# One more half of an FFN by Strassen's quarter products, and the modulation sums laid out anew over three FFNs

## What is computed

```python
cond = jax.nn.silu(c)
for i in range(DEPTH):
    mod = (cond @ ada_w[i] + ada_b[i]).reshape(b_, N_SUBLAYERS, 3, D_MODEL)
    h = adaln(x, norm_g[i, 0], mod[:, 0, 0], mod[:, 0, 1])
    x = x + 0.5 * (1.0 + mod[:, 0, 2][:, None, :]) * swiglu(h, ffn_w_in[i, 0], ffn_w_out[i, 0])
    ...
def swiglu(h, w_in, w_out):
    g, u = jnp.split(h @ w_in, 2, axis=-1)
    return (jax.nn.silu(g) * u) @ w_out
```

## Time and profile before

| | |
|---|---|
| median of three runs | 2896.82 us |
| profiled execution | 2896.0 us |
| its span | 2893.6 us (2.4 us lie around it) |
| PE busy | 2873.8 us (99%) |
| DVE busy | 1939.4 us (67%) |
| ACT busy | 1264.7 us (44%) |
| granted TensorE clock, mean | 0.999 |

### The profile page before, as it was taken

One profiled execution on the slowest core, in us unless ns is written; L12 is line 12 of the kernel. 1 busy time (PEld: TensorE's weight loads), 2 busy tenths in 40 slices (PEclk: granted clock), 3 DMA queues, 4 the chain that ended last, 5 costly groups with the idle time before them and its releaser, 6 DMA issues. The chain is left out here.

```text
span 2893.6 us, 40922 instructions
## 1 busy us (share of the span) xinstructions
PE 2873.8 (99%) x16099; PEld 2485.7 (86%) x16099; DVE 1939.4 (67%) x2624; ACT 1264.7 (44%) x1752; POOL 144.9 (5%) x297
## 2 busy tenths in 40 slices
PE   8999999999999999999999999999999999999999
PEld 7888889899898998868999988788888888888887
DVE  8667688777786777876856758766535467754453
ACT  4223255344452445474533445654414348443332
POOL 0111100100001001040000000200000001000000
PEclk9999999999999999999999999999999999999999
DMA  7867613524236243251332322413232222232231
GB/s 299 272 217 255 210 45 115 206 109 154 89 115 230 91 168 107 88 182 61 108 126 79 114 91 88 160 63 110 87 105 98 95 81 95 96 108 95 88 109 66
DMA packets 100944, 366.99 MB, mean 127 GB/s; under 512 B 11248, under 2 KB 11808, under 8 KB 100784
## 3 DMA queue, kind: packets, MB, share of 16 engines
q1 hardware_dynamic: 77616, 276.56, 27.9%
q0 software_dynamic: 23168, 88.17, 8.8%
HBM read 362.51 MB, written 2.18 MB: 126 GB/s over the span
## 5 line engine op out<-in xcount | busy, mean ns | idle before, releaser
L1263 DVE TENSOR_TENSOR wl<-raw,wh 128x1024 fp32r<-128x1024 f32 x393 | 477.1, 1226 | 519.4 <-ACT wh L697 518.9
L697 ACT ACTIVATE wh<-raw 128x1024 fp32r<-128x1024 f32 x393 | 409.8, 1054 | 752.4 <-PE PS L2131 685.1
L2131 PE MATMUL PS<-HH,wh 128*128 128x512 f32 x1560 | 608.2, 390 | 0.4 <-DVE HL L1979 0.3
L2131 PE MATMUL PS<-HL,wh 128*128 128x512 f32 x1560 | 607.7, 390 | 0.0
L2131 PE MATMUL PS<-HH,wl 128*128 128x512 f32 x1560 | 607.7, 390 | 0.0
L2131 PEld LDWEIGHTS PS<-HH,wh 128*128 128x128 f32 x1560 | 293.1, 188 | 62.1 <-DVE HL L1979 0.8
L2131 PEld LDWEIGHTS PS<-HH,wl 128*128 128x128 f32 x1560 | 293.0, 188 | 60.5
L2131 PEld LDWEIGHTS PS<-HL,wh 128*128 128x128 f32 x1560 | 293.1, 188 | 60.3
L2131 PE MATMUL PS<-AH,wh 128*128 128x512 f32 x848 | 330.7, 390 | 0.5 <-DVEq L2014 0.5
L2131 PE MATMUL PS<-AL,wh 128*128 128x512 f32 x848 | 330.5, 390 | 0.0
L2131 PE MATMUL PS<-AH,wl 128*128 128x512 f32 x848 | 330.3, 390 | 0.0
(11 more groups left out here) (346 smaller groups left out, 5107.6 us busy)
## 6 DMA issues: line engine op xcount, KB each, us to landing
raw<-in_stream SPq DMA_DIRECT2D x459, 512.0 KB, 3.4
acc<-in_stream POOLq DMA_DIRECT2D x54, 512.0 KB, 4.9
WK<-in_stream SPq DMA_DIRECT2D x42, 512.0 KB, 4.5
piece<-in_stream POOLq DMA_DIRECT2D x38, 512.0 KB, 5.0
WK<-in_stream POOLq DMA_DIRECT2D x24, 512.0 KB, 6.6
arena<-in_stream SPq DMA_DIRECT2D x16, 512.0 KB, 12.5
HT<-in_stream POOLq DMA_DIRECT2D x12, 512.0 KB, 6.8
TBa<-negcum POOLq DMA_DIRECT2D x8, 640.0 KB, 5.0
```

The source lines that it names most:

```text
L697: F(wh[:, r, :], raw[:, r, :], ACT.Copy).then_inc(hi_done, 1)
L1263: TT(wl[:, r, :], raw[:, r, :], wh[:, r, :].bitcast(F32), ALU.subtract).then_inc(lo_done, 1)
L2131: mm = MM(PS[g % 2][:, j, :], l, x, start=(first and i == 0), stop=(last and i == 2), skip_group_check=after_halves)
```

## The change

The second half of the first FFN (`gate=0`) makes its five groups of the first map by quarter products. The mixtures of its input are made by ACT and DVE during the first half's groups 2 to 5 (`u` in the code), in `arena`, `acc`, `HT` and the places in `TH`, `TL` and `HH`/`HL`.

The 128 modulation sums are divided anew. The first FFN makes 64: 32 in groups 2 to 5 of the first half (two after each split), 22 in that half's output projection (three after each split), 10 in the second's (two after each split). The FFNs with gates 2 and 3 make 32 each, 22 and 10. The first 32 sums use a ring of three tiles in `WK` and `piece`, all others the ring of four. The second half's groups of the first FFN have no sums.

Small moves go with it: the broadcast condition vector `condc` lives in `bands` until the end of the first FFN, so the load of the pooling bands is issued there by SP and not at the start; the scratch of two small reductions is `SG` instead of `WK`.

```diff
--- before.py
+++ after.py
@@ -76,13 +76,13 @@
 
-FAST = {2: (4, 5), 3: (4, 5), 5: (4, 5)}
-
-ADA_BY = {0: 8 + 3 * NADA, 2: 8 + 4 * NADA, 3: 8 + 5 * NADA}
-
-ADA_EARLY = ADA_BY[0]
-
-ADA_PHASES = (16, 8)
+FAST = {0: (0, 5), 2: (4, 5), 3: (4, 5), 5: (4, 5)}
+
+ADA_EARLY = 32
+
+ADA_PHASES = (22, 10)
+
+ADA_BY = {0: ADA_EARLY + 32, 2: ADA_EARLY + 64, 3: ADA_EARLY + 96}
 
@@ -178,6 +178,7 @@
                                             tile=2 * (ng - nf), sums=ADA_BY[f["gate"]] - ADA_PHASES[1] if late else 0))
+                    st["at"][half] = st["parts"][-1]
                 add["fs"] += 7 * nf
@@ -283,7 +284,7 @@
                     *(WK[:, 2 * i:2 * i + 2, :].rearrange("p k t -> p (k t)") for i in range(2))]
-        ada_tiles = [acc[:, 1, 1024:2048], acc[:, 1, 2048:3072], piece[:, 0:1024]]
+        ada_tiles = [ada_late[2], ada_late[3], ada_late[0]]
 
@@ -330,9 +331,13 @@
 
-        def mix_raw(i):
-
-            o = 2048 + 1024 * i + (2048 if i >= 4 else 0)
+        def mix_raw(i, sets):
+
+            if sets == 0 and i == 7:
+                return HT[:, :, :].rearrange("p a (b t) -> p (a b) t", b=2)
+            if sets == 0 and i >= 4:
+                return acc[:, 1, 1024 * (i - 4):1024 * (i - 3)].rearrange("p (k t) -> p k t", k=4)
+            o = ((4096, 5120, 10240, 11264)[i] if sets == 0 else 2048 + 1024 * i + (2048 if i >= 4 else 0))
             return arena[:, o:o + 1024].rearrange("p (k t) -> p k t", k=4)
@@ -590,6 +594,11 @@
                     loaded = part["c"] + RING
+                if st is plan[2]:
+                    load_chunks(loaded, part["c"] + st["halves"][1][1] + 1)
+                    loaded = part["c"] + st["halves"][1][1] + 1
+                    sp.wait_ge(cond_moved, 1)
+                    sp.dma_start(bands[:, 0:NBAND], A["params"][:, NCOL:NCOL + NBAND]).then_inc(bands_in, 16)
             load_chunks(loaded, NCH)
@@ -611,15 +620,18 @@
             pl.memset(ones[:, :], 1.0).then_inc(ones_done, 1)
-            pl.wait_ge(ada0_step, 14)
+            pl.wait_ge(ht_done, KT)
             for m, (s, j) in enumerate(ADA_ORDER[:ADA_EARLY]):
...
             for st in plan:
-                for part, n in zip(st.get("parts", ()) if st.get("gate") in ADA_BY else (), ADA_PHASES):
-                    pl.wait_ge(a_ready, part["e"] + part["n"] + 1)
+                for part, n in zip(st["at"] if st["kind"] == "ffn" and st["gate"] in ADA_BY else (), ADA_PHASES):
+                    if part:
+                        pl.wait_ge(a_ready, part["e"] + part["n"] + 1)
+                    else:
+                        pl.wait_ge(mix_ready, 4)
                     for i in range(n):
@@ -888,7 +900,7 @@
                 act.wait_ge(mix_sum, 4 * sets + i + 1)
-                src = mix_raw(4 + i)
+                src = mix_raw(4 + i, sets)
                 if i < 3:
@@ -1003,7 +1014,11 @@
                                 split_until(c + 4 * u + 8)
+                                if u == 4:
+                                    for i in range(3):
+                                        mix_high(i, st["sets"])
                                 hidden_group(st, e + u, g + u, c + 4 * (u + 1), cv + u, j + u, 2 * u, 0)
+                            mix_high(3, st["sets"])
                             e, cv, g, c, j, pairs = e + ng, cv + ng, g + ng, c + 4 * ng, j + ng, 0
@@ -1025,6 +1040,9 @@
                                 split_until(c + nt // 2 + RING)
+                                if st is plan[2] and c + nt == c_last:
+                                    act.wait_ge(ada_step, ADA_BY[0])
+                                    F(condb, condc, ACT.Copy).then_inc(cond_moved, 1)
                             c += nt // 2
@@ -1621,22 +1639,25 @@
-            def whole(k, t, i):
-
-                link(TT(mix_raw(i), quadrant(HH, k, t).bitcast(F32), quadrant(HL, k, t).bitcast(F32), ALU.add))
-
-            def mixed_input(i, a, b, op):
+            def whole(k, t, i, sets):
+
+                link(TT(mix_raw(i, sets), quadrant(HH, k, t).bitcast(F32), quadrant(HL, k, t).bitcast(F32), ALU.add))
+
+            def mixed_input(i, sets):
...
-                if op is None:
-                    STT(mix_raw(4 + i), a, -1.0, b, ALU.mult, ALU.subtract).then_inc(mix_sum, 1)
+                if i >= 2:
+                    dve.wait_ge(mix_sum, 4 * sets + (1 if i == 2 else 3))
+                a, b = (mix_raw(k, sets) for k in ((0, 1), (1, 2), (4, 2), (3, 6))[i])
+                if i == 2:
+                    STT(mix_raw(4 + i, sets), a, -1.0, b, ALU.mult, ALU.subtract).then_inc(mix_sum, 1)
...
-                    TT(mix_raw(4 + i), a, b, op).then_inc(mix_sum, 1)
+                    TT(mix_raw(4 + i, sets), a, b, ALU.add if i == 3 else ALU.subtract).then_inc(mix_sum, 1)
...
-                src = mix_raw(4 + i)
+                src = mix_raw(4 + i, sets)
@@ -1773,51 +1794,62 @@
...
-                        if ada and not st["parts"]:
-                            paired = st is plan[2] and c == st["c"]
-                            if paired:
-                                split_until(c + 10)
-                                hidden_group(st, e, g, cv, j, 0, 0)
-                                split_until(c + 11)
-                                hidden_group(st, e + 1, g + 1, cv + 1, j + 1, 2, 0)
-                                split_until(c + 12)
-                                e, cv, g, c, j = e + 2, cv + 2, g + 2, c + 8, j + 2
-                            for u in range(2 if paired else 0, ng):
+                                fast_groups(st, part, None)
+                            e, cv, g, c, j, ng = e + ng, cv + ng, g + ng, part["c"], j + ng, 0
+                        elif st is plan[2]:
+                            split_until(c + 10)
+                            hidden_group(st, e, g, cv, j, 0, 0)
+                            split_until(c + 11)
+                            hidden_group(st, e + 1, g + 1, cv + 1, j + 1, 2, 0)
+                            split_until(c + 12)
+                            e, cv, g, c, j = e + 2, cv + 2, g + 2, c + 8, j + 2
+                            for u in range(2, ng):
                                 for i in range(4):
                                     split_until(c + RING + 1 + i)
-                                    n = (2 if i < 3 else 1) if st is plan[2] else 1 if i < 3 else 2
-                                    ada_until(min(ada, at["ada"] + n))
+                                    ada_until(at["ada"] + 2)
+                                    if (u, i) == (2, 1):
+                                        whole(0, 0, 0, sets)
+                                        whole(0, 1, 1, sets)
+                                        mixed_input(0, sets)
+                                    elif (u, i) == (2, 3):
+                                        whole(1, 1, 2, sets)
+                                    elif (u, i) == (3, 1):
+                                        mixed_input(1, sets)
+                                        mixed_input(2, sets)
+                                    elif (u, i) == (3, 3):
+                                        whole(1, 0, 3, sets)
+                                        mixed_input(3, sets)
+                                    elif u == 4 and i:
+                                        mix_low(i - 1, sets)
                                 hidden_group(st, e, g, cv, j, 2 * u, 0)
                                 e, cv, g, c, j = e + 1, cv + 1, g + 1, c + 4, j + 1
-                            ada_until(min(ada, at["ada"] + 1))
-                            if paired:
-                                late_constants()
-                        pairs = 0 if ada or st["parts"] else ng // 2
+                            mix_low(3, sets)
+                            late_constants()
+                        pairs = 0 if part or st is plan[2] else ng // 2
                         with dve.Fori(0, pairs) if pairs else nullcontext(0) as it:
                             for u in range(2) if pairs else ():
                                 base = at["split"]
@@ -1834,9 +1866,11 @@
                             else:
-                                splits_with_sums(c + nt // 2 + RING, 2 if st["parts"] else 1, ada or at["ada"])
-                                if half == 1 and st["parts"]:
-                                    fast_groups(st, st["parts"][1],
+                                ahead = c + nt != c_last and st["at"][1]
+                                splits_with_sums(c + nt // 2 + RING, 3 if ahead else 2,
+                                                 0 if ada is None else ada - ADA_PHASES[1] if ahead else ada)
+                                if half == 1 and ahead:
+                                    fast_groups(st, ahead,
                                                 lambda: add_out(st, g, c + nt // 2, 4, gate))
```

(26 more changed lines are left out.)

48 lines of the change are left out of this document (21 added, 27 removed).

## The result

The changed kernel takes 2905.76 us (median of 10 runs, 2901.51 to 2909.67) against 2896.43 (10 runs, 2895.98 to 2897.84): ratio 1.0029, 95% interval 1.0021 to 1.0037. It is slower by 0.3%, 9.3 us. 2898.3 was forecast, in a range of 2889.5 to 2907, with a chance of 0.21 for slower. The profiled execution took 2906.0 us; its span is 2904.1, 10.5 more than the span before.

A forecast was written before the change was run, and what follows sets the result against it. PE, busy for 2873.8 of 2893.6 us, was taken to bound the kernel. Terms -8.0 (quarter products), +9.0 (first FFN pauses) and +0.5 (gates 2 and 3) gave +1.5 us, median 2898.3, range 2889.5 to 2907.

The forecast's parts named there:

- The quarter products: First FFN's second half, five groups of the first map: 108.8 us becomes 100.8, a gain of 8.0 us.
- The larger gain: Same five groups: by the skill's gap for an isolated matmul, the change would bring 11.8 us; not adopted.
- The first FFN up to its quarter products: DVE's sums and mixtures run late: 2.2 us pause behind group 5, projection ends 5.9 us late, at 220.2.
- Before the quarter products: First FFN, ahead of the first three quarter products: PE pauses of 0.9, 0.5 and 3.2 us, waiting for `wl`.
- the list itself: Row-by-row account of DVE, ACT, POOL and PE in the first FFN: pauses of 10.5 us with median landings; 9.0 charged.
- Gates 2 and 3: FFNs with 22 sums for 16 before their quarter products: 0.5 us charged for both together.
- 590.8 as the point where a pause begins: Gates 2 and 3: PE pauses if the last sum ends after 590.8; the list ends it at 589.7 to 590.5.
- what holds PE up lengthens it one for one: Whole kernel: PE is the bound, so each pause of PE adds its own length to the time.
- the likeliest case: Whole kernel: pauses about eat the gain, median 2898.3, own range 2892 to 2902.6, chance 0.52.
- Rival B: Slower: POOL's landings grow to 6.5 us in the projections, first FFN pauses 14.2 us; +8.8, 2906; chance 0.21.
- Its deciding point: Rival B decides once all pauses together pass 13.8 us (8.0 + 5.8).
- Edits at nothing: Two more sums per second projection, the `condc` copy, the bands' load, sums leaving the first FFN: charged no time.

The follow-up runs named there:

- e4_half: Changed kernel with half the bytes (256 KB) in 29 of 32 modulation tiles of the first FFN's groups 2 to 5, 29 values wrong: 2903.02 us.
- e6_early: Changed kernel with late constants moved to the second projection, weight quarters asked for after the 20th sum, three of POOL's first four loads issued earlier: 2893.66 us.
- e2_wait20: Changed kernel with the load of the first weight quarters waiting for the 20th of the 22 sums instead of the 22nd: 2895.82 us, ratio 0.9997.
- e7_early18: e6_early with 18 and 14 sums in the first and second output projections of the three FFNs instead of 22 and 10: 2906.61 us, ratio 1.0038.
- e8_18: e2_wait20 with 18 and 14 sums in the first and second output projections of the three FFNs instead of 22 and 10: 2903.03 us, ratio 1.0023.
- e5_ceiling: Changed kernel with late constants moved to the second projection and 12 of the 22 sums left out in each of three FFNs: 2891.21 us, ratio 0.9983.

## Why the prediction was right and where it was not

**The quarter products** (8.0 us): right, 7.96 measured. The larger gain, which the prediction worked out as an estimate from the isolated gap in the Trainium skill, "TensorE: Matmul & The Clock Gate", section "Back-to-back issue gap" (11.8 us; its own figures give 11.9), did not come.

**The first FFN up to its quarter products:** right in mechanism and place. `mix_low` ended at 168.2 (167.1 was forecast), the split at 174.2 (173.0), pause 2.9 (2.2), last sum 214.4 (215.0), end of the projection 5.6 late (5.9). But the last number is right by luck, from two errors: 3.7 us were to come from 5.7 us of DVE for each chunk, and 3.4 came from the longer first pause (0.9 with its overlap), the clock (1.7), the 0.5 from the start and 0.3 in small pieces. Landings in this projection were 5.4 in the median, 5.7 taken. e4_half and e6_early show the chunk-by-chunk lag where the first pause is gone.

**Before the quarter products:** 4.85 us of pause for 4.6. So the first FFN's pauses came to 7.8 us where 9.0 were charged (the list itself gave 10.5); with clock and overlap it lost 12.1.

**Gates 2 and 3** (0.5 in all): mis-sized, 3.4 us of pause, 5.3 with clock and overlap. With gate 2 the last sum came 0.8 to 1.6 us later than the list followed by rows had it (596.0 less the 4.6 that all is late here: 591.3), and SP's first quarter landed 5.2 us after its issue where I had taken the 3.7 of the earlier trace rows, the least of six. With gate 3 the first quarter landed after 3.6 us, so there the late sum alone made the pause of 1.28. With 590.8 as the point where a pause begins, the term stood at its edge and should have been charged with the spread of what comes before it. (The row at 604.70, given as the third `wl`, is the fourth product's; the third's is the one ahead of it, whose end lies at 604.8, so nothing in the sum hangs on this.)

**The step that failed: "what holds PE up lengthens it one for one".** The sum took every pause at its own length. The six of the changed kernel cost 5.7 us beyond it, 4.7 through the clock. Of the 8.4 us between the account's 9.9 and the 1.5 forecast, that is 5.7; pauses of 11.2 for 9.5 are 1.7, the start is 0.5, and small pieces are the rest. Pauses alone, +11.2 + 0.5 - 8.0 = +3.7 us, would have been the likeliest case; with the clock the medians are 9.3 apart, and it is slower. That the measured time lies in the stated range is owed to the range's far end, which was put there for longer landings and not for the clock. Rival B had the right sign and nearly the number (2906), with a mechanism that is not what happened in the first FFN: its landings of 6.5 us were measured at 5.4. Its deciding point, pauses of 13.8 us, was not reached either; the clock made up for it. What it shares with the likeliest case, the weight quarters' load held by the 22nd sum, is what e2_wait20 shows to carry the loss.

**Edits at nothing:** no pause lies in the five groups or at the bands and `condc`. That two more sums fit each second projection holds (no pause there); e7_early18 and e8_18 show that four further ones do not fit with gates 2 and 3.

## What to carry to other kernels

A buffer that is shared between two uses makes a deadline of the last operation of the first use: ask which operation really frees it. Here waiting for the 20th sum instead of the 22nd was worth 9.9 us, more than the algorithmic gain. Where two causes hold the same engine at the same place (constants, and loads asked for late), removing either moves the pause and only both remove it, so test the pair. And a pause of TensorE, where it bounds the kernel, can cost more than its length: 5.7 us more for 11.2 us of pauses here.

## What the runs showed of the hardware

TensorE's clock fell behind all of the pauses of 2.5 us and more in the FFNs' traces (2.52, 2.82, 2.94, 3.06, 3.37, 3.79 and 4.11 among them: granted 0.85 to 0.92 over the next 20 us, 1.5 to 3 us lost). It stayed at 1.00 behind those of 1.28, 1.33, 1.43, 1.68 and 2.31. Between 2.0 and 2.4 it went either way: 2.03 (e4_half) and 2.10 (the changed kernel) with gate 2 were followed by 0.91; 2.02 (e4_half, at 204), 2.05 (e7_early18, gate 2) and 2.12 (e5_ceiling) by 1.00; and the pause of 2.41 at 17 us by 0.83 in the window 15 to 25 of the changed kernel and by 1.00 in that of e7_early18. Nor does the length of one pause decide alone: in the mixer behind the first FFN every trace, that of before too, has short pauses in a row (0.3 to 1.65 us) and a low clock; over 385 to 425 it is 0.96 before and in the changed kernel and 0.91 in e5_ceiling and e7_early18. The low clock can begin at once (174.43) or 1.5 us after PE has started again (231.15, 232.66).

That PE falls to half its clock when idle stands in the Trainium skill, "TensorE: Matmul & The Clock Gate", section "Part 1: The HAM clock gate (the "warmup" mystery)"; the traces agree, 0.43 us for a matmul that takes 0.2267.

A modulation tile of 512 KB landed 5.4 us after POOL issued it in the median of the first projection, where the DMA engines were 0.97 busy from 174 to 194, and never under 3.5. The estimate of 3.2 us that follows from the Trainium skill, "DMA: Bandwidth & Descriptors", section "Anatomy of one DMA — SWDGE (gpsimd) path", does not hold there.
